# Tuned two-block transformer kernel: the dilated attention scores its keys once, in four planes, and the last stages leave out tokens that the output does not hold

## The reference, cut to what matters

```python
DIL_CONFIGS = ((128, 1), (512, 4), (2048, 16))
def _dilated_group(q, k, v, window, dilation, slopes):
    # query t attends to t + j*dilation, |j| <= window/(2*dilation)
    ...
    bias = -slopes[:, None, None] * dist[None]
    scores = einsum(q, k) * (E ** -0.5) + bias
    scores = where(valid, scores, MASK_VALUE)
    lse = logsumexp(scores); p = exp(scores - lse); o = einsum(p, v)
    return o, lse
# the three groups are merged by weights softmax(lse) over the groups
```

```python
def conv_ffn(x, w_up, conv_w, w_down):
    u = causal_dwconv(x @ w_up, conv_w)      # token t reads t, t-1, t-2
    gate, val = jnp.split(u, 2, axis=-1)
    return (jax.nn.silu(gate) * val) @ w_down
...
    return h[:, N_META:]                     # the meta tokens are not returned
```

## Time and profile before

| | us |
|---|---|
| median of 3 runs | 3845.82 (3841.38 to 3847.10) |
| the profiled execution, its own time | 3846.73 |
| its span, first to last instruction | 3844.7 |
| TensorE busy with matmuls | 3685.3 (96%) |
| DVE busy | 1951.2 (51%) |
| ACT busy | 1329.8 (35%) |
| POOL busy | 151.6 (4%) |
| mean granted TensorE clock | 0.976 of full |
| moved from and to memory | 81 GB/s mean |

### The profile page before, as it was taken

One profiled execution on the slowest core, in us unless ns is written; L12 is line 12 of the kernel. 1 busy time (PEld: TensorE's weight loads), 2 busy tenths in 40 slices (PEclk: granted clock), 3 DMA queues, 4 the chain that ended last, 5 costly groups with the idle time before them and its releaser, 6 DMA issues. The chain is left out here.

```text
span 3844.7 us, 57861 instructions
## 1 busy us (share of the span) xinstructions
PE 3685.3 (96%) x22661; PEld 3224.8 (84%) x22661; DVE 1951.2 (51%) x2813; ACT 1329.8 (35%) x1980; POOL 151.6 (4%) x180
## 2 busy tenths in 40 slices
PE   8999899999999999999899989988999899889998
PEld 7888788888888887787788869988999887689998
DVE  3334853335333666666733345555664355656653
ACT  3222542224222433333432235544333333333332
POOL 1000010001000100000100010001000100010001
PEclk9999999999999999999899989989999999989999
DMA  4233222332333222221133322211223221012232
GB/s 134 95 104 96 91 83 89 105 102 77 98 98 102 79 66 72 66 72 61 55 94 98 104 66 72 67 55 61 93 87 99 66 73 39 28 55 88 93 99 72
DMA packets 89985, 312.71 MB, mean 81 GB/s; under 512 B 10832, under 2 KB 15312, under 8 KB 89696
## 3 DMA queue, kind: packets, MB, share of 16 engines
q1 hardware_dynamic: 89344, 308.24, 24.7%
q0 software_dynamic: 480, 2.17, 0.2%
HBM read 308.27 MB, written 2.10 MB: 81 GB/s over the span
## 5 line engine op out<-in xcount | busy, mean ns | idle before, releaser
L624 PE MATMUL ps<-x_hi,w_hi 128*128 128x264 f32 (+2 forms) x3952 | 1351.7, 342 | 14.1 <-DVE x_lo L1980 6.5
L624 PE MATMUL ps<-x_hi,w_lo 128*128 128x264 f32 (+2 forms) x3952 | 1334.8, 338 | 0.0
L624 PE MATMUL ps<-x_lo,w_hi 128*128 128x264 f32 (+2 forms) x3952 | 1331.1, 337 | 0.0
L1672 DVE TENSOR_TENSOR w_lo<-raw,w_hi 128x1024 fp32r<-128x1024 f32 x579 | 706.4, 1228 | 361.4 <-ACT w_hi L1155 352.4
L624 PEld LDWEIGHTS ps<-x_hi,w_hi 128*128 128x128 f32 x3952 | 746.2, 189 | 118.0 <-issue 23.9
L624 PEld LDWEIGHTS ps<-x_lo,w_hi 128*128 128x128 f32 x3952 | 744.7, 188 | 80.6
L624 PEld LDWEIGHTS ps<-x_hi,w_lo 128*128 128x128 f32 x3952 | 746.3, 189 | 77.6
L624 PE MATMUL ps<-h_hi,w_hi 128*128 128x264 f32 (+2 forms) x1992 | 650.4, 327 | 6.1 <-issue 3.9
L624 PE MATMUL ps<-h_hi,w_lo 128*128 128x264 f32 (+2 forms) x1992 | 641.2, 322 | 0.0
L624 PE MATMUL ps<-h_lo,w_hi 128*128 128x264 f32 (+2 forms) x1992 | 639.3, 321 | 0.0
L1155 ACT ACTIVATE w_hi<-raw 128x1024 fp32r<-128x1024 f32 x579 | 602.9, 1051 | 103.2 <-PE ps L624 95.3
(11 more groups left out here) (229 smaller groups left out, 3163.6 us busy)
## 6 DMA issues: line engine op xcount, KB each, us to landing
raw<-wstream SPq DMA_DIRECT2D x579, 512.0 KB, 3.4
res<-xT SPq DMA_DIRECT2D x8, 256.0 KB, 7.4
out<-res SPq DMA_DIRECT2D x4, 264.0 KB, 2.2
invc<-consts POOLq DMA_DIRECT2D x1, 1024.0 KB, 5.6
out<-res SPq DMA_DIRECT2D x4, 248.0 KB, 2.1
bias<-consts POOLq DMA_DIRECT2D x1, 512.0 KB, 3.8
g_chunk<-consts POOLq DMA_DIRECT2D x1, 264.0 KB, 3.0
g_keep<-consts POOLq DMA_DIRECT2D x1, 256.0 KB, 3.1
```

Source lines behind the costliest of these rows:

```text
L624: m = pe.matmul(ps[:, bank, 0:n], w[:, slot, wt, :], x[:, k, c0:c0 + n], start=first and q == 0, stop=last and q == 2)
L1672: dve.tensor_tensor(w_lo[:, slot], raw[:, slot], w_hi[:, slot].bitcast(F32), ALU.subtract)\
```

## The change

The change has two parts.

**Attention.** The scores are computed once, with the keys on the partitions, in four planes of 128 x 512 (plane 0 and 1 the two dilated groups, planes 2 and 3 the even and the odd blocks of the near group); every plane has the queries in the same order, by residue. DVE adds the bias into `scored` and takes the elementwise maximum over the planes (`over_keys`). TensorE transposes that maximum (eight transposes), DVE reduces it out of PSUM, and eight transposes widen it. DVE subtracts the widened maximum from `scored`, and ACT takes the exponentials in place. The second set of scores, `far`, `joint`, and half of `widen` are gone. `weigh` now has stationary operands of 64 columns, values into one bank and ones into another, both heads side by side on the partitions, so that `normalise` is one reciprocal and one product on 128 partitions. The bias table is 128 x 2048 in place of 128 x 1024. q of group 0 is now also stored by residue (ACT `take`, j = 0).

**Trimmed tokens.** In the last `project2` of the attention and the last `glu2`, 516 columns (`TAIL`, tokens from 12 on) are computed in place of 528, as two halves of 258; after the convolution and in the last down projection it is the 512 returned tokens, one bank of 512 columns in place of two of 264, and halves of 256 for the last tile.

The diff, cut to its core:

```diff
+TAIL = S + 4
...
-    project2(KD, (KD,), 4, "norm11", "norm12")
-    ffn2(1, 0, "norm13")
+    project2(KD, (KD,), 4, TAIL, "norm11", "norm12")
+    ffn2(1, 0, TAIL, S, "norm13")
...
         def two_banks(tok):
-            return tok == T
+            return tok > S
...
-            return (h * (T // 2), T // 2) if two_banks(tok) else (META + h * (S // 2), S // 2)
+            return T - tok + h * (tok // 2), tok // 2
...
+                def scores(p, plane):
+                    if plane == 0:
+                        pe.wait_ge(s_evac, st["t0"] + 9 * p + 6)
+                    if plane < 2 and p >= 1:
+                        pe.wait_ge(A["x"], 4 * p)
+                    if plane >= 2:
+                        pe.wait_ge(A["add"], 8 * p + 2 * plane - 2)
...
+                def turn_maxima(p):
+                    for half in range(2):
+                        pe.wait_ge(A["max"], 6 * p + 5 + half)
+                        for r in range(R4):
+                            m = pe.transpose(ps[:, 2 + half, r * P:(r + 1) * P], over_keys[:, half, r * P:(r + 1) * P],
+                                             ident[:, :])
+                        m.then_inc(A["turn"], 1)
...
+                    def both(cols, weights, moving, start, stop):
+                        for bank, what in ((6, weights), (7, lambda half: ones[:, :])):
+                            for half in range(2):
+                                m = pe.matmul(cols(ps[head(half), bank, :]), what(half), moving(half),
+                                              start=start, stop=stop, skip_group_check=True)
...
                 def second_part(p, t):
-                    if t in (4, 8, 13, 18):
-                        scores_turned(p, (4, 8, 13, 18).index(t))
-                    if t == 24:
-                        weigh(p, 0, False)
-                    if t == 30:
-                        weigh(p, 0, True)
-                    if t == 33:
-                        weigh(p, 1, False)
-                    if t == 36:
-                        weigh(p, 1, True)
+                    if t == 3:
+                        turn_maxima(p)
+                        turn_values(p, 2)
+                    if t == 9:
+                        widen(p)
+                    if t == 27:
+                        weigh(p, False)
+                        weigh(p, True)
...
-                            if slot in (51, 54, 57, 61):
-                                scores(p, (51, 54, 57, 61).index(slot))
+                            if slot == 51:
+                                scores(p, 0)
+                                scores(p, 1)
                             if slot == 59:
                                 turn_values(p, 0)
-                            if slot == 66:
+                                scores(p, 2)
+                                scores(p, 3)
+                            if slot == 68:
                                 turn_values(p, 1)
-                            if slot == 70:
-                                widen(p)
...
+                def maxima(p, plane):
+                    for half in range(2):
+                        dve.wait_ge(A["add"], 8 * p + 2 * plane + half + 1)
+                        top, x = over_keys[:, half, :], scored[:, half, plane, :]
+                        if plane == 1:
+                            if p >= 1:
+                                dve.wait_ge(A["turn"], 2 * p - 1 + half)
+                            dve.tensor_tensor(top, scored[:, half, 0, :], x, ALU.max).then_inc(A["max"], 1)
+                            continue
...
-                    dve.reciprocal(recip[o, :], ps[total, 6 + half, :]).then_inc(A["rec"], 1)
+                    dve.reciprocal(recip[:, :], ps[:, 7, :]).then_inc(A["rec"], 1)
```

More of the change, by code:

```diff
@@ L85 @@
 C_BIAS = C_POOL + 4 * S
[L86 to L87 removed]
+N_BIAS = 4 * S
 C_SLOPE = C_BIAS + N_BIAS
@@ L110, in constants @@
     same = np.where(steps % 4 == 0, -4.0 * steps, MASKED)
-    far = np.concatenate([near * (slopes[HEADS] / slopes[0]), same * (slopes[2 * HEADS] / slopes[0])], axis=1)
-    c[:, C_BIAS + 2 * WIN:C_BIAS + 4 * WIN] = np.tile(far, (1, 2))
+    query = np.arange(S).reshape(NI, R4).T.reshape(1, S)
+    planes = [np.tile(near * (slopes[HEADS] / slopes[0]), (1, R4)),
+              np.tile(same * (slopes[2 * HEADS] / slopes[0]), (1, R4))]
+    for odd in range(2):
+        first = query // R4 < (80 if odd else 48)
+        dist = np.abs(query - np.where(first, P * odd, P * odd + 2 * P) - i)
+        planes.append(np.where(dist <= DIL[0][0], -dist, MASKED))
+    c[:, C_BIAS:C_BIAS + N_BIAS] = np.concatenate(planes, axis=1)
     c[:, C_SLOPE:C_SLOPE + HEADS] = slopes[:HEADS]
@@ L340, in build @@
         qk = at("qk", [P, 2, 6, S])
-        val = at("val", [P, R4, 3, 3 * HD])
+        val = at("val", [P, R4, 3, P])
+        ones = at("ones", [P, HD])
         vT = at("vT", [P, 2, S])
[L343 to L348, removed]
+        scored = at("scored", [P, 2, 4, S])
+        over_keys = at("over_keys", [P, 2, S])
+        top_q = at("top_q", [P, 2, R4])
+        bias = at("bias", [P, 4, S])
         recip = at("recip", [P, S])
@@ L526, in window, with by_query, near_cols, score_bank @@
             return max(P * b - HD, 0), min(P * b + P + HD, S)
[L528 to L548, removed]
+        def by_query(ap):
+            return ap.rearrange("p (r i) -> p r i", r=R4)
+        def near_cols(plane):
+            return slice(0, 112) if plane == 2 else slice(16, NI)
+        def score_bank(plane, half):
+            return 2 + 2 * (plane % 2) + half
         def attend_bank(w):
@@ L811, in turn_values @@
                     m.then_inc(A["vtr"], 1)
-                def chunk(p, c, swap, done):
-                    buf = p % 2
[L816 to L821, removed]
-                                own, other = (k, q) if swap else (q, k)
-                            else:
-                                lo, hi = window(what)
-                                own = qk[hs, buf, swap, P * what:P * what + P]
-                                other = qk[hs, buf, 1 - swap, lo:hi]
-                            m = pe.matmul(ps[:, score_bank(c, half), at_:at_ + n], own, other, start=True, stop=True)
-                    m.then_inc(done, 1)
@@ L871, in weigh @@
                         return
[L872 to L879 removed]
+                    pe.wait_ge(A["exp"], 4 * p + 4)
@@ L880, in weigh @@
+                    for b in range(R4):
+                        lo, hi = window(b)
+                        m = both(lambda out: by_query(out)[:, :, lo // R4:hi // R4],
+                                 lambda half: val[:, b, 0, head(half)],
+                                 lambda half: by_query(scored[:, half, 2 + b % 2, :])[:, :, lo // R4:hi // R4],
+                                 False, b == 3)
                     m.then_inc(A["pv"], 1)
                 def second_part(p, t):
-                    if t in (4, 8, 13, 18):
-                        scores_turned(p, (4, 8, 13, 18).index(t))
@@ L1851, in attend1 @@
             def attend1(st):
-                def head(half):
-                    return slice(HD * half, HD * half + HD)
                 def slope(p, half):
```

361 lines of the change are left out of this document (152 added, 209 removed).

## The result

The changed kernel takes 3783.89 us (median of 4 runs, 3781.84 to 3786.74) against 3845.36 us for the kernel before on the same chip (4 runs, 3841.38 to 3847.10). The ratio is 0.9842, with a 95% interval of 0.9826 to 0.9857: faster by 61.5 us. The forecast was 3785.5 us.

A forecast was written before the change was run, and what follows sets the result against it. TensorE's matmul list was taken to bound the attention. Terms 34.2 + 6.6 + 1.7 - 1.0 - 0.5 + 6.2 + 13.1 = 60.3 us, from 3846.7 to 3786.4; the median 0.9 lower gives 3785.5 us, range 3774 to 3806.

The forecast's parts named there:

- TensorE's list bounds the stretch: Attention beside its units: TensorE is busy for all of 482.7 us, so whatever leaves its matmul list shortens the time.
- The second scores: Attention pairs: dropping two dilated and two near score groups saves 4.88 us a pair, 34.2 us over seven pairs.
- the merged groups: First scores in two groups in place of four: fixed parts of 0.83 us a pair go, 6.6 us over eight.
- The product: Values product of a pair: 6.75 us against 6.60 before, heads side by side; -1.0 us over seven pairs.
- Rival A: Values product: weight loads set the pace; total time 3812 us, or 3837 if heads did not overlap; chance 0.12.
- The hand-overs: DVE and ACT results reach TensorE in time in each pair: no wait, 2 us of room in the tightest place.
- Rival B: TensorE waits at the transposes of the maxima or at `widen`, 1 to 3 us a pair; about 3800 us; chance 0.12.
- To the end of the last unit: Everything up to the end of the attention's last unit: forecast gain 41.0 us.
- The term of -0.5 us: ACT storing q of group 0 with a stride may show at the first unit, costing 0.5 us.
- The tail: From the attention's last unit matmul to the projection: 21.5 us in place of 27.9, a gain put at 6.2 us.
- The trim: Trimmed tokens in the last stages: 13.1 us saved, of it 5.6 in `glu2`; bounds 7 and 14.
- Rival D: Last stages: trimming tokens does nothing because a narrow matmul's cost is fixed; total time 3797 us; chance 0.02.

## Why the prediction was right, step by step

**TensorE's list bounds the stretch.** Right: 0.9 us of waiting in 490 us, at the first full unit, and the pair shrank by 5.64 us where the steps had promised 5.56.

**The second scores and the merged groups.** Right. The merged groups are confirmed by themselves (0.84 us measured for 0.83). The 4.88 us for the second scores are confirmed only by the pair as a whole; no run put them back alone.

**The product.** Right, 6.86 us for 6.75. Rival A was the case to fear: with the heads apart the pair is 5.16 us longer. The Trainium skill ("TensorE: Matmul & The Clock Gate", What happens when you issue a matmul) gives some 81 ns for 128 columns in a stream of weight loads and matmuls; the traces show 54 ns a record with the heads in turn and 110 with them apart, so neither order agrees with it, and the estimate of 3799 us made from it fell. The rows of `fox` were the right guide.

**The hand-overs.** Right, and too careful. The bound of 0.69 us for each operation of 448 columns left 2 us of room in the tightest place; they took 0.62 to 0.68 in the mean. More than that, the two stores and two weight splits that I had set between the last scores and the maxima are the most that could fall there; one store did. DVE was done 5.6 us after it had begun (1571.36 to 1576.93), TensorE needed what was ready another 7.7 us later, and the sum had left 2.2. Rival B was further off than its chance of 0.12 says.

**To the end of the last unit.** 42.4 us for 41.0. Seven pairs explain 39.5, so 2.9 lie in the start and in what left the loop, forecast at 0.83 + 1.7 - 0.5 = 2.0. The term of -0.5 us failed: q of group 0 stored with a stride was to delay the first unit, but TensorE waits there for 0.87 us in the kernel before as in the changed one. Another 0.3 us had been gained before the attention began.

**The tail was mis-sized**: 8.3 us for 6.2 (the prediction's own working, 27.9 - 21.5, gives 6.4). "So the product takes 6.75 + 2.6 us" took the half clock for longer than it lasted: four records took 0.43 us only until 1783.8, 3.3 us, and from the product's start to the reciprocal it was 8.31 us against 9.4. The product began 6.2 us behind the last unit matmul, not 6.8, and reciprocal to projection took 5.1, not 5.3. What remains is that the two waits do cost clock: 1.5 us in the product and 1.5 in the projection, which the runs with added matmuls took back.

**The trim was mis-sized**, 9.7 us in the trimmed stages for 13.1, and the term that failed is the `glu2`: "2112 matmuls lose 6 columns each, 5.6 us". The stage went from 268.5 to 266.6 us: 1.9 us. Part of that is the execution: in the window of 50 us of the three profiles with 264 columns 414, 416 and 416 matmuls start, in nine with 258 columns 419 (four times), 420 and 422 (four times). The means are 415.3 and 420.4, so 0.1204 and 0.1189 us a matmul: 1.5 ns for six columns, 3.1 us in all, where 2.65 ns were forecast. The whole stage gives the same, 268.6 us in the mean of three profiles and 265.5 in the mean of ten. So the profiled pair understates the term, and the forecast overstates it. Why the six columns buy less than 0.44 ns each, and what sets the pace of an execution, stays open; where the columns start was tested and is not it. The other terms held: the projection gave 1.3 us (62.3 to 61.0) for 1.0, and the down part with its end 6.4 (143.1 to 136.7) for 6.5, 5.5 of it in the seven full tiles (15.33 us a tile). The stages between the tail and the last projection, whose instructions are the same in all kernels here, lasted from 1520.5 to 1527.8 us in thirteen profiles, so the 10.8 us of the whole remainder say less than these rows. Rival D's time has a slip: without the 13.1 us the run would be 3798.6 and not 3797.

**The balance.** The errors of +1.4, +2.1 and -2.3 us nearly cancel, and the last of them would be -3.4 without the 1.1 us from stages that nothing touched; the forecast of 3785.5 is 1.6 us off by more luck than its terms had. The tail and the trim lie within the bounds that were stated for them.

## What to carry to other kernels

When one engine is busy through a whole stretch, price a change to its list by the distance between its neighbours' starts, group by group: columns and the fixed part of a group (0.4 us here) are separate prices. Look for another place of the same kernel where the new form of instruction already runs; the 0.22 us of `fox` for four records decided a question worth 5 us a pair. Here a matmul that fills half the array was cheap (54 ns a record) only beside one that fills the other half (110 ns otherwise), so the order of the two is part of the change: some 45 of the 61.5 us hang on it.

## What the runs showed that was not expected

- **A long wait costs twice.** A wait of 7.8 us was followed by about 3 us lost at a granted clock of 0.50. The wait of 5.15 us ahead of the projection was followed by a loss of 1.3 to 2.2 us in nine profiles, against the 9.4 us for 40 matmuls without it, so even the same wait has no fixed price.
- **Two profiles of one program differ in one loop.** The last `glu2` started 419 matmuls in 50 us in one profile of the changed kernel and 422 in another; over its 2112 matmuls that is 1.8 us, with the same clock and no wait in that window of either. A term of 2 us there can't be read from one pair of profiles.
- **Idle work was worth having.** Matmuls that nobody reads, in the waits of the tail, gave 3.0 us by the rows; the whole runs can't tell it from the changed kernel.
